# Norming queries and keys of a latent attention: squares on ScalarE, norm weights in tables and evictions, the query's factor in the softmax scale

## The reference

```python
def rms_norm(x, gain):
    return x * rsqrt(mean(x * x, axis=-1) + EPS) * gain

q = (rms_norm(q_lat, q_lat_norm) @ w_q_up).reshape(B, S, H, 192)
kv = (rms_norm(kv_lat, kv_lat_norm) @ w_kv_up).reshape(B, S, H, 256)
k = concatenate([kv[..., :128], k_rope for every head])
q, k = rms_norm(q, q_norm), rms_norm(k, k_norm)
q = concatenate([q[..., :128], rotary(q[..., 128:], cos, sin)])   # k likewise
s = q @ k.T * 192 ** -0.5        # masked by chunks of 64
out = softmax(s) @ v
```

## Time and profile before

| | |
|---|---|
| median of 3 runs | 1569.75 us (1569.43 to 1570.15) |
| span of the profiled execution, first to last instruction | 1568.1 us (median less span: 1.65 us) |
| mean granted TensorE clock over the span | 0.982 |
| busy: PE, PEld, DVE, ACT, POOL | 94%, 76%, 50%, 38%, 41% |

### The profile page before, as it was taken

The page is one execution under the profiler, slowest core; times in us unless marked ns, Lnnn a source line. Parts: engine busy times, 40 slices in busy tenths (PEclk is TensorE's granted clock), DMA queues, the critical chain, the costliest instruction groups (busy, mean ns, idle before and its releaser), DMA issues. The chain is left out here.

```text
span 1568.1 us, 18614 instructions
## 1 busy us (share of the span) xinstructions
PE 1477.2 (94%) x6967; PEld 1196.0 (76%) x6967; DVE 783.0 (50%) x1505; ACT 596.9 (38%) x1053; POOL 638.7 (41%) x338
## 2 busy tenths in 40 slices
PE   6997889999999999999989898889999999999997
PEld 5886657787788888888868775678867888888886
DVE  4289468335376504653133965772345663055620
ACT  5524554457433212232154146633564322122220
POOL 5433621453343444444335254423523444444342
PEclk9998999999999999999999899999999999999999
DMA  5322001332233233333143220012322332333321
GB/s 146 96 80 68 27 1 41 94 108 68 81 94 94 88 101 95 94 94 100 35 118 95 68 81 1 1 65 84 118 68 70 95 106 88 90 106 89 99 87 74
DMA packets 172975, 125.81 MB, mean 80 GB/s; under 512 B 11825, under 2 KB 149840, under 8 KB 172880
## 3 DMA queue, kind: packets, MB, share of 16 engines
q1 hardware_dynamic: 172880, 124.56, 26.7%
HBM read 122.44 MB, written 2.10 MB: 79 GB/s over the span
## 5 line engine op out<-in xcount | busy, mean ns | idle before, releaser
L552 POOL TENSOR_TENSOR w_lo<-raw,w_hi 128x1024 fp32r<-128x1024 f32 (+2 forms) x230 | 544.5, 2371 | 789.2 <-ACT w_hi L938 789.1
L938 ACT ACTIVATE w_hi<-raw 128x1024 fp32r<-128x1024 f32 (+2 forms) x230 | 236.7, 1033 | 354.6 <-PE bank L599 349.0
L597 PE MATMUL bank<-x_hi,w_hi 128*128 128x512 f32 (+1 forms) x880 | 349.7, 397 | 0.3 <-DVE x_lo L1221 0.3
L598 PE MATMUL bank<-x_lo,w_hi 128*128 128x512 f32 (+1 forms) x880 | 347.8, 395 | 0.0
L599 PE MATMUL bank<-x_hi,w_lo 128*128 128x512 f32 (+1 forms) x880 | 347.8, 395 | 0.0
L597 PEld LDWEIGHTS bank<-x_hi,w_hi 128*128 128x128 f32 (+1 forms) x880 | 164.7, 187 | 41.7 <-issue 1.0
L598 PEld LDWEIGHTS bank<-x_lo,w_hi 128*128 128x128 f32 (+1 forms) x880 | 164.7, 187 | 41.0 <-issue 1.0
L599 PEld LDWEIGHTS bank<-x_hi,w_lo 128*128 128x128 f32 (+1 forms) x880 | 164.7, 187 | 40.7
L597 PE MATMUL bank<-w_hi,x_hi 128*128 128x512 f32 (+1 forms) x448 | 168.7, 376 | 18.7 <-POOL w_lo L552 12.5
L1289 DVE TENSOR_TENSOR h<-h,bank 128x512 f32<-128x512 f32 x64 | 44.0, 688 | 250.3 <-PE bank L599 250.2
L599 PE MATMUL bank<-w_hi,x_lo 128*128 128x512 f32 (+1 forms) x448 | 165.2, 369 | 0.0
(11 more groups left out here) (266 smaller groups left out, 1930.6 us busy)
## 6 DMA issues: line engine op xcount, KB each, us to landing
raw<-in_w_ffn_in SPq DMA_DIRECT2D x88, 512.0 KB, 3.8
raw<-in_w_ffn_out SPq DMA_DIRECT2D x40, 512.0 KB, 3.7
raw<-in_w_in SPq DMA_DIRECT2D x36, 512.0 KB, 3.7
raw<-in_w_mix_out SPq DMA_DIRECT2D x16, 512.0 KB, 3.8
raw<-in_w_ca_kv SPq DMA_DIRECT2D x32, 256.0 KB, 3.3
raw<-in_w_ca_q SPq DMA_DIRECT2D x8, 512.0 KB, 3.9
raw<-in_w_ca_out SPq DMA_DIRECT2D x8, 512.0 KB, 3.8
h<-in_x SPq DMA_DIRECT2D x4, 512.0 KB, 5.0
```

The lines of the kernel that those rows point to most:

```text
L552: pool.tensor_tensor(w_lo[i % SPLIT][:, 0:n], raw[i % RAW][:, 0:n], w_hi[i % SPLIT][:, 0:n].bitcast(f32), ALU.subtract).then_inc(S["lo_spl ...
L597: pe.matmul(o, ah, bh, start=first, stop=False)
L598: pe.matmul(o, ah, bl, start=False, stop=False)
L938: act_.activation(w_hi[k % SPLIT][:, 0:n], raw[k % RAW][:, 0:n], ACT.Copy).then_inc(S["hi_split"], 1)
```

## The change

- **Squares.** ScalarE squares whole blocks of queries (`q_sq`, 768 columns) and of the keys' 128-channel parts (`k_sq`, 512 columns); VectorE sums them with one or two reductions per block in place of the eight square-and-sum pairs.
- **Queries' factor.** Queries are no longer multiplied by their factor. It becomes the scale of the exponential: sum + 192 EPS is raised to the power -1/2, which holds the 192 ** -0.5 of the softmax too. The scaled negative maximum takes it as well.
- **Norm weights.** For the 128 unrotated channels the product of the query's and the key's weight is one column, applied when ScalarE evicts the transposed keys. For the 64 rotary channels GpSimd multiplies the sine and cosine tables by the weights, 8 products per layer, after slab q_up 1.
- **Shared rotary key.** It is squared, summed and rotated once for all heads and blocks (`shared_rope_key`); each key block then multiplies it by the heads' factors while it spreads it.
- **Order.** VectorE's key blocks run one behind: the sums of block i, then the products of block i - 1.
- Before the loop: two transfers of the first 128 weights with channels on the partitions, one product for both layers. The program is built with a descriptor scratch of 1024 bytes.

The diff, cut:

```diff
+                for i, name in enumerate(("mla_q_norm", "mla_k_norm")):
+                    sp.dma_start(nope_gains[:, i, :], A[name][:, 0:NOPE].rearrange("l p -> p l"),
+                                 allow_slow_non_contiguous=True).then_inc(S["nope_in"], 16)
                 for name, (r0, n) in rows_of.items():
...
                 dve.tensor_copy(pair_mask[:, :, :], pairs[:, :, :])
+                dve.wait_ge(S["nope_in"], 32)
+                dve.tensor_tensor(gains_all[:, :, ROWS], nope_gains[:, 0, :], nope_gains[:, 1, :], ALU.mult)
...
+                    if i == slab_at["q_up", 1]:
+                        pool.wait_ge(S["spread_in"], 16 * (1 + len(spread_of)))
+                        for z, name in enumerate(("mla_q_norm", "mla_k_norm")):
...
+                            for j, (g_, table) in enumerate(((g1, cos), (g2, sin), (g2, cos), (g1, sin))):
+                                pool.tensor_tensor(rot_tab[:, 4 * z + j], table[:, :, :], g_, ALU.mult
+                                                   ).then_inc(S["tab_done"], 1)
...
+                act_.wait_ge(S["lat_ss_mm"], 1)
+                for t in range(NT):
+                    act_.wait_ge(S["q_evac"], NT + t + 1)
+                    act_.activation(q_sq[:, t, :], q_tok[:, t, :], ACT.Square).then_inc(S["sq_done"], 1)
                 ahead(("kv_up", 0))
...
+                for t in range(NT):
+                    act_.wait_ge(S["k_evac"], t + 1)
+                    act_.activation(k_sq[:, t, :].rearrange("p (r h x) -> p r h x", r=2, h=2), nope_of(k_tok, t), ACT.Square
+                                    ).then_inc(S["sq_done"], 1)
...
                     act_.wait_ge(S["qk_ss"], n + 1)
-                    inverse_rms(small[:, c + 128:c + 132], small[:, c + 96:c + 100], small[:, c + 64:c + 68], QK, S["qk_r"])
+                    if n < NT:
+
+                        link(act_.activation(small[:, c + 96:c + 100], small[:, c + 64:c + 68], ACT.Ln, bias=eps_c[:, 2:3]))
+                        act_.activation(small[:, c + 128:c + 132], small[:, c + 96:c + 100], ACT.Exp, scale=-0.5).then_inc(S["qk_r"], 1)
+                    else:
+                        inverse_rms(small[:, c + 128:c + 132], small[:, c + 96:c + 100], small[:, c + 64:c + 68], QK, S["qk_r"])
...
-                                        ACT.Copy).then_inc(S["qkT_evac"], 1)
+                                        ACT.Copy, scale=gain("mla_qk_nope", 0) if z else 1.0).then_inc(S["qkT_evac"], 1)
...
-                attend(0, MLA_GROUPS, lambda t: (t + 1) * P, lambda hd, t: QK ** -0.5, [probsT], probs, first_queries)
+                attend(0, MLA_GROUPS, lambda t: (t + 1) * P, lambda hd, t: small[:, R_QK + 128 + 4 * t + hd:R_QK + 129 + 4 * t + hd],
+                       [probsT], probs, first_queries)
...
-                            if causal:
-                                ng = dve.tensor_scalar(small[:, st + 32:st + 32 + len(g_)], small[:, st:st + len(g_)], -scale, None, ALU.mult)
-                            else:
...
+                            ng = dve.scalar_tensor_tensor(small[:, st + 32:st + 32 + len(g_)], small[:, st:st + len(g_)], -1.0,
+                                                          small[:, c:c + 4 * len(g_) - 3:4], ALU.mult, ALU.mult)
...
-                def prepare(z, t):
...
+                def rotate(x1, x2, tabs, tmp, done):
+                    dve.tensor_tensor(tmp[0], x1, tabs[0], ALU.mult)
+                    dve.tensor_tensor(tmp[1], x2, tabs[1], ALU.mult)
+                    dve.tensor_tensor(tmp[2], x2, tabs[2], ALU.mult)
+                    link(dve.tensor_tensor(tmp[3], x1, tabs[3], ALU.mult))
+                    dve.tensor_tensor(done[0], tmp[0], tmp[1], ALU.subtract)
+                    return dve.tensor_tensor(done[1], tmp[2], tmp[3], ALU.add)
...
+                def query(t):
+                    c = R_QK + 4 * t
+                    dve.wait_ge(S["sq_done"], t + 1)
+                    dve.tensor_reduce(four(c), nope_of(q_sq, t), AX.X, ALU.add)
+                    link(dve.tensor_reduce(four(c + 32), rope_of(q_sq, t), AX.X, ALU.add))
                     dve.tensor_tensor(small[:, c + 64:c + 68], small[:, c:c + 4], small[:, c + 32:c + 36], ALU.add
                                       ).then_inc(S["qk_ss"], 1)
...
+                    dve.wait_ge(S["tab_done"], 4)
...
+                def shared_rope_key():
+                    dve.wait_ge(S["rope_evac"], 1)
+                    dve.wait_ge(S["tab_done"], 8)
...
+                def key_squares(t):
+                    c = R_QK + 4 * (NT + t)
+                    dve.wait_ge(S["sq_done"], NT + t + 1)
+                    link(dve.tensor_reduce(small[:, c:c + 4], k_sq[:, t, :].rearrange("p (h x) -> p h x", h=NH), AX.X, ALU.add))
+                    dve.tensor_scalar(small[:, c + 64:c + 68], small[:, c:c + 4], small[:, R_KR + t:R_KR + t + 1], None, ALU.add
+                                      ).then_inc(S["qk_ss"], 1)
...
+                def key(t):
+                    nope, rope = nope_of(k_tok, t), rope_of(k_tok, t)
+                    dve.wait_ge(S["qk_r"], NT + t + 1)
...
                     dve.tensor_tensor(nope, nope, factor.to_broadcast([P, 2, 2, NOPE]), ALU.mult)
...
+                    dve.tensor_tensor(rope, kr_rot[:, t, :].unsqueeze(1).unsqueeze(1).to_broadcast([P, 2, 2, ROPE]),
+                                      factor.to_broadcast([P, 2, 2, ROPE]), ALU.mult).then_inc(S["qk_done"], 1)
...
+                def prepare(i):
+                    if i < NT:
+                        query(i)
+                        if i == NT - 1:
+                            shared_rope_key()
+                    else:
+                        key_squares(i - NT)
+                        if i > NT:
+                            key(i - NT - 1)
+                        if i == 2 * NT - 1:
+                            key(NT - 1)
...
-    nc = bacc.Bacc("TRN2", target_bir_lowering=False, num_devices=1)
+    nc = bacc.Bacc("TRN2", target_bir_lowering=False, num_devices=1, dynamic_dma_scratch_size=1024)
```

More of the change, by code:

```diff
@@ L203, in build_trunk @@
         kr_tok = sb("kr_tok", [P, NT, ROPE])
-        small = sb("small", [P, 548])
+        small = sb("small", [P, 556])
         KB = 1024
@@ L234, in build_trunk @@
         q_tok, k_tok = place("q_tok", R3, [P, NT, NH * QK]), place("k_tok", R3 + 12, [P, NT, NH * QK])
+        q_sq = place("q_sq", R1, [P, NT, NH * QK])
+        k_sq = place("k_sq", R0 + 8, [P, NT, NH * NOPE])
         Qx = [[place(f"Qx{x}_{i}", kb + 8 * x, [P, NH, SEQ]) for i, kb in enumerate((R3 + 4, R0))] for x in range(2)]
@@ L1315, in _ @@
                 dve.wait_ge(S["spread_in"], 16 * (1 + len(spread_of)))
-                def prepare(z, t):
-                    tok, name = (q_tok, "mla_q_norm") if z == 0 else (k_tok, "mla_k_norm")
-                    nope, rope = nope_of(tok, t), rope_of(tok, t)
-                    c = R_QK + 4 * (z * NT + t)
-                    if z:
-                        dve.wait_ge(S["k_evac"], t + 1)
-                        dve.wait_ge(S["rope_evac"], 1)
-                        link(dve.tensor_copy(rope, kr_tok[:, t, :].unsqueeze(1).unsqueeze(1).to_broadcast([P, 2, 2, ROPE])))
-                    else:
-                        dve.wait_ge(S["q_evac"], NT + t + 1)
-                    for hd in range(NH):
-                        for part, x, n in ((nope, 0, NOPE), (rope, NOPE, ROPE)):
-                            head = part[:, hd // 2, hd % 2, :]
-                            col = c + hd + (32 if x else 0)
-                            last = dve.tensor_tensor_reduce(out=junk_v[:, hd, x:x + n], in0=head, in1=head, scale=1.0, scalar=0.0,
-                                                            op0=ALU.mult, op1=ALU.add, accum_out=small[:, col:col + 1])
-                    link(last)
@@ new lines, in query @@
+                    halves = rope[:, :, :, 0:R2_], rope[:, :, :, R2_:ROPE]
+                    dve.wait_ge(S["tab_done"], 4)
+                    rot = r_diag[:, :, :].rearrange("p a (r h x) -> p a r h x", r=2, h=2)
+                    rotate(*halves, [rot_tab[:, j, t, :].unsqueeze(1).unsqueeze(1).to_broadcast([P, 2, 2, R2_]) for j in range(4)],
+                           [rot[:, j] for j in range(4)], halves).then_inc(S["qk_done"], 1)
+                    dve.wait_ge(S["qk_done"], t + 1)
+                def shared_rope_key():
+                    dve.wait_ge(S["rope_evac"], 1)
+                    dve.wait_ge(S["tab_done"], 8)
+                    halves = kr_tok[:, :, 0:R2_], kr_tok[:, :, R2_:ROPE]
+                    link(rotate(*halves, [rot_tab[:, 4 + j] for j in range(4)], [kr_tmp[:, j] for j in range(4)],
+                                (kr_rot[:, :, 0:R2_], kr_rot[:, :, R2_:ROPE])))
+                    sq = kr_tmp[:, 0:2].rearrange("p a t x -> p (a t x)").rearrange("p (t x) -> p t x", t=NT)
+                    link(dve.tensor_tensor(sq, kr_tok[:, :, :], kr_tok[:, :, :], ALU.mult))
```

(2 more changed lines are left out.)

58 lines of the change are left out of this document (27 added, 31 removed).

## The result

The changed kernel takes **1529.65 us** (median of 4 runs, 1528.90 to 1531.09); the kernel before took 1569.59 beside it (4 runs). The ratio is 0.9743 [0.9732, 0.9755]: 40 us less, where 24 were forecast (1545.7, range 1541 to 1557).

A forecast was written before the change was run, and what follows sets the result against it. VectorE's pace per query block was taken to hold back ScalarE's weight splits and starve TensorE. -27.69 + 0.9 + 0.9 + 1.8 = -24.1 us against the 1568.1 us span, plus 1.65, gave 1545.7 us, range 1541 to 1557.

The forecast's parts named there:

- the section: First feature chunk to query transposes, each layer: 72.62 us instead of 86.43 and 86.50, saving 27.69 us in all.
- the start: SyncE's queue: two small transfers ahead of norm rows and x delay TensorE's first norm transposes, +0.9 us once.
- the key evictions: ScalarE's 8 evictions of transposed keys, scaled by a per-partition column, pay 0.114 us more each: +0.9 us.
- the softmax: Attention's exponentials on ScalarE with a per-partition column as scale: +1.8 us, half of a possible 3.65.
- VectorE's block: VectorE's query work per 128-query block in the section, with the feature eviction: 3.7 us instead of 8.69.
- a catch: A VectorE instruction held up by GpSimd's low half; one per slab makes VectorE's period 5.9 us, absorbed by the cover.
- first rival (the lock): In the section, VectorE or ScalarE still falls behind through GpSimd's shared-port lock, two catches per slab: 1557 us, chance 0.14.
- VectorE in the attention: The small product for the negative maximum takes another form: nothing; bounds 1 us either way.
- own sign of being wrong: A section above 78 us, waits for kv_up's low half, or an attention stage over 2 us a layer longer.
- The 32 exponentials: Attention's exponentials on ScalarE, each 0.114 us longer with a column as scale; half counted, 1.8 of 3.65 us.
- Squares: ScalarE's four query and four key squares in the section, at most 0.83 us each, are covered: nothing paid.
- Tables: GpSimd's eight table products per layer, 0.42 us each, 3.4 together, fit in 7.2 us of room: nothing paid.

The follow-up runs named there:

- before's distance: The changed kernel with the arena 192 bytes higher, so x lies 192 modulo 256 bytes from the weights as in the kernel before: 1553.64 us, ratio to before 0.9891.

## Why the prediction was wrong, and where it was right

- **The failed step: a term that is missing.** The sum is the section, the start, the key evictions and the softmax; all the rest of both layers stands in it at nothing, without a reason. The prediction asks what the change removes, adds and moves among instructions, and says of the smaller scratch "touches no transfer of this program"; of five new or wider tiles it counts the work that fills them, never where they push the others. That rest measured -18.1 us, by a spacing of 226.7 ns for 228.9 to 233.3. By itself the shift of the operands was worth 19.7 us in the old kernel (1569.4 to 1549.7) and 24.0 in the new one (1553.6 to 1529.6). No rival had it either. The trace of before did show that something was there: products of one shape were 233.3 ns apart with x moving and 228.9 with the weights moving. A distance between operands can't be read from a row, but it can be added up from the tiles of the two kernels.
- **The section was right.** 72.62 us were forecast, 72.60 measured at before's distance and 72.0 at the new one, at a clock of 1.0, with ScalarE waiting for TensorE's release. VectorE's block: forecast 3.7, or 5.9 with a catch; measured 4.9 (87.74 to 92.62) within 5.44, a catch of 1.9 in it, covered. Its account of the parts was too even: the queries' half does nearly all of it. Its first rival (the lock) was there and covered, as it said.
- **Wrong size: VectorE in the attention, "nothing; bounds 1 us either way".** It is +7 in the stage (5.1 between the medians): the two-operand form is held by GpSimd for 1.0, 0.6 and 1.5 us at the start of the stage, and TensorE's clock falls behind it. The step knew that either form can be held up and did not ask how often: the one-operand 128x1 took 0.153 us on average in before, never held. The prediction's own sign of being wrong, an attention stage longer by more than 2 us a layer, came true (3.1 and 4.0).
- **The 32 exponentials, +1.8 forecast: about 0.** They are longer by 0.088 us (128x256, 0.466 to 0.554), not 0.114, and with them in place the stage took 42.7 us as before. The Trainium skill (ScalarE: Activation LUTs, What ACT_TABLE_LOAD costs) gives 93 ns for a per-partition operand, which was nearer than the row of another tile that I took; none of it shows in the stage.
- **Key evictions** 0.9 forecast, 0.4 measured: 0.08 us longer each (621 to 702 ns), two thirds of it on the path. **Squares**: covered, no TensorE wait for a low half. **Tables**: 0.46 us each, overlapping, 3.4 us for the eight (57.79 to 61.14), as forecast, and not paid. **Start**: +0.9 as forecast in the profiled run; 0.7 to 2.5 us in the other kernels with the transfers first, from -0.1 to +0.6 with them last (8.03 to 8.79 us after the first transpose, 8.17 in before).

At before's distance the forecast would have been 8 us too low (1553.6), inside the range. The profiled execution of that run was its slowest, with a span 10.8 us above the forecast one: 6.4 of it is the attention stage (46.98 and 46.83 us), 2.3 the output matrix at 233.3 ns, 1.6 the start, and the remaining 0.5 the sum of small differences of both signs.

## What to carry to other kernels

When a change adds or widens a tile, work out where the operands of the hot products land before and after, and read the spacing of equal products in a stage that the change does not touch; here the distance between stationary and moving operand modulo 256 bytes was worth 1.3%, and 64 unused bytes gave it. When a scalar factor moves to a place beside a busy GpSimd, count how often its small product will be held for GpSimd's whole instruction, and what TensorE's clock does behind it. Of two symmetric halves of a change, try each alone: here the queries were the bottleneck, and the keys were under cover.

## What was not expected of the hardware

- The spacing of f32r products of 128x512 depends on the distance of the two operands: 226.7 ns at 0 modulo 256, in every kernel that had it, 228.9 to 234.3 ns at the six other distances run; 0 and 256 are alike, and no other pair was tried for a period. At one and the same distance (192) the products with weights moving ran at 228.9 ns in the kernel before and at 231.2 on average in the changed one, and at 64 those with x moving at 228.9 in one layer and 233.3 in the other, so a second condition remains that was not found.
- For 256 columns the order is another: 120.0 ns at distance 0, some 117 at 192 (before), and at 64 113.5 in one kernel and 117.8 in another.
- A VectorE addition of 4 columns took 0.16 us or 1.9 us, by whether GpSimd's subtraction ran beside it.
